# Newest block first on ScalarE, the gate's silu in one group, the finished features rounded behind the last head, the last panel turned by half

## The chip, the cores and the metric

One core of a Trainium2 chip runs the whole program. TensorE (PE) does the matmuls and transposes, ScalarE (ACT) the activations and copies, VectorE (DVE) the elementwise work and reductions, GpSimd (POOL) some elementwise work, and SyncE (SP) issues the DMAs. The metric is the device time of one execution, in microseconds (us); lower is better.

## What is computed

Two transformer blocks on 1024 tokens of width 1024, float32 in and out. The change lies in the last three stages of the second block: multi-head latent attention and the output product.

```
    q = (rms_norm(c_q, q_a_norm) @ w_uq).reshape(B, L, MLA_HEADS, QK_HEAD)
    kv = (rms_norm(c_kv, kv_a_norm) @ w_ukv).reshape(B, L, MLA_HEADS, QK_NOPE + V_HEAD)
    k_nope, v = kv[..., :QK_NOPE], kv[..., QK_NOPE:]
    k = jnp.concatenate([k_nope, k_r], axis=-1)
    q = rms_norm(q, q_norm)
    k = rms_norm(k, k_norm)
...
        s = jnp.einsum('bqhd,bkhd->bhqk', qb, k).astype(jnp.float32) * scale
        mask = cid[None, :] <= qc[:, None]
        s = jnp.where(mask[None, None], s, neg)
        p = jax.nn.softmax(s, axis=-1).astype(v.dtype)
        return jnp.einsum('bhqk,bkhd->bqhd', p, v)
...
    return o * jax.nn.silu(z)
...
    y = jnp.concatenate([y_conv, y_mla, y_ret], axis=-1)      # 256 + 512 + 256 features
    h = h + y @ w_out[l]
```

y has 256 features of the convolution, 512 of the attention (8 heads of 64) and 256 of the retention.

Float32 products are made of three matmuls on operands rounded to a shorter float32 format (F32R): high by high, high by low, low by high. "Rounding" a tensor means a copy to its high part on ScalarE and the difference, its low part, on VectorE.

## The kernel before

Every engine has its own instruction stream, written out by hand; semaphores (counted steps) are the only order between engines. Weights come in panels. A panel is loaded (`sp_weights`, line 285), rounded on ScalarE (`act_split`, line 294) and on VectorE (`dve_split`, line 300), and multiplied by `pe_dense` (lines 313 to 315): per half of 512 tokens 8 blocks k of input features, 3 matmuls each, so 24 matmuls of 512 columns a half and 48 a panel. The three stages that matter:

**Latent stage.** Its last four panels `mz` 0 to 3 (the gate z) have matmuls enough to hide other work behind, which is put into *slots* between the k blocks. `slot_at` names the blocks after which a slot comes: 3 slots in each of the halves 0 to 2, 4 in each of the halves 3 to 5, 7 in the halves 6 and 7. Slots 0 to 16 start one *item* each: item m = 0 to 7 is the query product of a block of 128 tokens (12 matmuls of 384 columns, line 2376), item m = 8 to 16 the key and value product of a block (6 matmuls of 512 columns, line 2386; the last block has 16 tokens). An item goes through steps s = 0 to 3, one slot apart: s = 0 is the product on TensorE and on ScalarE its copy out of PSUM (lines 2400, or 2416 and 2417) and the square (2402, 2419); s = 1 the sum of squares on VectorE (2431, 2445 and 2447) and the square root on ScalarE (2405, 2423); s = 2 the normalisation on VectorE; s = 3 the rope on GpSimd. In one slot every engine does its part of up to four items, and `head_slots` lists them **oldest item first**. An item's two PSUM banks come from a ring of four, so TensorE's item m needs the copies of item m - 2. The results are stored to HBM (lines 2471, 2475) and, when all stores have landed, loaded again by head (`head_sp`, lines 2483 to 2485). `silu(j - 1)` of the gate runs at the start of panel mz j on ScalarE (line 2239). The halves 6 and 7 hold the preparation of head 0: its first step transposes the loaded queries (tile `qhd`, line 326).

**Attention stage.** For each of 8 heads 14 units (pairs of a key block and a query half): three score matmuls (2606 to 2608), exp on ScalarE (2654), one value matmul (2617). Behind the units of head h lies the preparation of head h + 1; behind head 7 lies nothing.

**Output stage.** The 8 feature blocks y (k = 0, 1 convolution, in `yb`; 2 to 5 attention, in `zf2`; 6, 7 retention, transposed from `rb`) are rounded into XH and XL (lines 2734, 2737, 2757), then 8 panels of `w_out_2` are multiplied, the residual `hr` is added (line 2765), the panel is transposed back (`turn`, line 326), copied to `ot` (line 2744) and stored (line 2846). Feature block 5 needs the end of head 7: a reciprocal on VectorE (line 2668) and two products on GpSimd.

## Time and profile before

| | us |
|---|---|
| median of 3 runs | 2192.44 (2191.07 to 2192.71) |
| the profiled execution | 2190.02 |
| its span, first to last record | 2188.1 |
| TensorE busy in it | 2045.3 (93%) |
| ScalarE, VectorE, GpSimd busy | 699.9, 1039.6, 381.5 |
| mean granted TensorE clock | 0.967 of 2.4 GHz |

TensorE is busy for 93% of the span, so a gain has to come from its idle stretches, from its time at the lower clock, or from what precedes and follows its work. A busy matmul overlaps the next one: one of 512 columns is recorded with 0.39 us while they start 0.23 us apart.

### The profile page before, as it was taken

The numbers are of one execution on the slowest core, as the hardware profiler recorded it, in microseconds if no ns is written. First come the engines' busy times: TensorE is split into PE (matmuls) and PEld (weight loads), VectorE is DVE, ScalarE is ACT, GpSimd is POOL, SyncE is SP. The second block draws the span as 40 slices with busy tenths as digits, with TensorE's granted clock in tenths as the row PEclk, the third lists the DMA queues.
The fourth block names the chain that finished last, engine by engine and source line by source line (L and its number), as shares of the span: only waits on it lengthen the run. The fifth ranks groups of instructions, "written<-read, shape, count | busy, mean of one in ns | idle before, by whom it ended". The sixth has DMA issues, their size and how long they took to land.

```text
span 2188.1 us, 24747 instructions
## 1 busy us (share of the span) xinstructions
PE 2045.3 (93%) x9965; PEld 1672.3 (76%) x9965; DVE 1039.6 (48%) x1700; ACT 699.9 (32%) x1204; POOL 381.5 (17%) x436
## 2 busy tenths in 40 slices
PE   7988799959998999999999999997989999799998
PEld 6766588847786888888888888775978897576677
DVE  5666734644545333333333335436454436566541
ACT  4435121234434212212112123334111126555421
POOL 3142201630030000000000002343051316000100
PEclk9989899969999999999999999998999999899999
DMA  4133232122111111111111111111310132411123
GB/s 140 39 95 117 77 100 79 55 72 58 49 46 46 49 49 49 49 49 48 46 51 40 50 56 58 38 39 52 117 38 20 49 106 97 134 44 30 39 77 96
DMA packets 195721, 139.18 MB, mean 64 GB/s; under 512 B 35016, under 2 KB 180680, under 8 KB 195096
## 3 DMA queue, kind: packets, MB, share of 16 engines
q1 hardware_dynamic: 195608, 137.60, 20.9%
q8 instruction: 79, 1.29, 0.3%
q14 instruction: 34, 0.28, 0.0%
HBM read 109.22 MB, written 28.36 MB: 63 GB/s over the span
## 4 chain that ended last, share of the span: by engine, by line
PE 79%; DVE 10%; ACT 5%; issue 2%; POOL 2%; DMA 1%; SPq 0%; ACTq 0%; DVEq 0%; POOLq 0%
PE ps L313 21%; PE ps L314 20%; PE ps L315 20%; PE ps L326 3%; PE ps L2617 3%; PE ps L517 2%; PE ps L1174 1%; DVE wlo L300 1%; PE ps L2547 1%; PE ps L2606 1%; PE ps L2607 1%; PE ps L2608 1%; DVE fm L910 1%; DVE xl L1442 1%; PE ps L1158 1%
## 5 line engine op out<-in xcount | busy, mean ns | idle before, releaser
L313 PE MATMUL ps<-xh,whi 128*128 128x512 f32 (+2 forms) x1728 | 694.3, 402 | 34.2 <-DVE wlo L300 18.4
L314 PE MATMUL ps<-xl,whi 128*128 128x512 f32 (+2 forms) x1728 | 674.8, 391 | 0.0
L315 PE MATMUL ps<-xh,wlo 128*128 128x512 f32 (+2 forms) x1728 | 671.3, 388 | 0.0
L313 PEld LDWEIGHTS ps<-xh,whi 128*128 128x128 f32 x1728 | 331.9, 192 | 109.7 <-issue 24.4
L315 PEld LDWEIGHTS ps<-xh,wlo 128*128 128x128 f32 x1728 | 331.2, 192 | 66.1
L314 PEld LDWEIGHTS ps<-xl,whi 128*128 128x128 f32 x1728 | 331.6, 192 | 61.4 <-issue 3.1
L294 ACT ACTIVATE whi<-wraw 128x1024 fp32r<-128x1024 f32 (+2 forms) x151 | 147.0, 974 | 360.6 <-PE ps L315 347.9
L300 DVE TENSOR_TENSOR wlo<-wraw,whi 128x1024 fp32r<-128x1024 f32 (+2 forms) x151 | 192.9, 1278 | 115.7 <-ACT whi L294 115.6
L313 PE MATMUL ps<-ffh,whi 128*128 128x512 f32 x512 | 199.4, 389 | 0.0
L314 PE MATMUL ps<-ffl,whi 128*128 128x512 f32 x512 | 199.3, 389 | 0.0
L315 PE MATMUL ps<-ffh,wlo 128*128 128x512 f32 x512 | 199.2, 389 | 0.0
L1508 DVE TENSOR_TENSOR hT<-hT,ps 128x512 f32<-128x512 f32 x128 | 87.7, 687 | 178.7 <-PE ps L315 178.7
L1412 POOL COPY acc<-sqp 128x512 f32<-128x512 f32 x6 | 3.5, 613 | 677.8 <-ACT sqp L1599 677.8
L1468 ACT ACTIVATE rr<-rr 128x512 f32<-128x512 f32 x64 | 40.5, 633 | 247.3 <-DVE rr L1487 247.3
L315 PEld LDWEIGHTS ps<-ffh,wlo 128*128 128x128 f32 x512 | 96.1, 188 | 20.1
L313 PEld LDWEIGHTS ps<-ffh,whi 128*128 128x128 f32 x512 | 96.1, 188 | 20.1
L314 PEld LDWEIGHTS ps<-ffl,whi 128*128 128x128 f32 x512 | 96.1, 188 | 19.8
L1487 DVE SCALAR_TENSOR_TENSOR rr<-ps,rst 128x512 f32<-128x512 f32 x64 | 44.2, 691 | 133.4 <-PE ps L315 133.4
L2617 PE MATMUL ps<-pt,vm 128*128 128x512 f32 (+4 forms) x224 | 89.8, 485 | 0.0
L1489 DVE TENSOR_TENSOR ffl<-rr,ffh 128x512 fp32r<-128x512 f32 x64 | 44.4, 693 | 87.2 <-ACT ffh L1472 87.2
L2654 ACT ACTIVATE pt<-ps 128x512 f32<-128x512 f32 (+4 forms) x112 | 52.9, 473 | 74.1 <-PE ps L2608 73.7
L1415 POOL TENSOR_TENSOR acc<-acc,sqp 128x512 f32<-128x512 f32 x42 | 60.2, 1462 | 39.4 <-ACT sqp L1599 39.4
(437 smaller groups left out, 2590.8 us busy)
## 6 DMA issues: line engine op xcount, KB each, us to landing
wraw<-w_in SPq DMA_DIRECT2D x47, 512.0 KB, 3.7
wraw<-w_up SPq DMA_DIRECT2D x32, 512.0 KB, 4.1
wraw<-w_down SPq DMA_DIRECT2D x32, 512.0 KB, 3.4
xt<-x SPq DMA_DIRECT2D x8, 512.0 KB, 7.0
wraw<-w_o SPq DMA_DIRECT2D x16, 256.0 KB, 3.0
xr<-x SPq DMA_DIRECT2D x8, 512.0 KB, 4.4
wraw<-w_ple_gate SPq DMA_DIRECT2D x8, 512.0 KB, 4.3
h_d<-hT SPq DMA_DIRECT2D x8, 512.0 KB, 3.3
```

Source lines behind the costliest of these rows:

```text
L294: act.activation(whi[i % 2][:, 0:n], raw[i % 2][:, 0:n], ACT.Copy).then_inc(*act_w.up(i))
L300: dve.tensor_tensor(wlo[i % 2][:, 0:n], raw[i % 2][:, 0:n], whi[i % 2][:, 0:n].bitcast(F32), ALU.subtract).then_inc(*dve_w.up(i))
L313: pe.matmul(out, h, xh[:, k, c0:c1_], start=(k == 0), stop=False)
L314: pe.matmul(out, h, xl[:, k, c0:c1_], start=False, stop=False)
L315: mm = pe.matmul(out, l, xh[:, k, c0:c1_], start=False, stop=(k == nk - 1))
L326: t = pe.transpose(out, in_, ident[0:p, 0:p])
L1415: pool.tensor_tensor(acc, acc, sq[:], ALU.add).then_inc(*done.up("sum", i))
L1487: dve.scalar_tensor_tensor(r[:], tile("up", g, f, c0), 0.0, RST[:, s], ALU.max, ALU.mult).then_inc(*dve_ml.up("ev", "up", g, f, c0))
L1489: dve.tensor_tensor(ffL[g % 2][:, f, s], r[:], ffH[g % 2][:, f, s].bitcast(F32), ALU.subtract).then_inc(*dve_ml.up("ff low", g, f, c0))
L1508: dve.tensor_tensor(d, d, tile("down", g, n, c0), ALU.add).then_inc(*dve_ml.up("ev", "down", g, n, c0))
L2617: pe.matmul(tile("o", h, hf)[:, c0:512], values_of(h, x), pts[j % 4][0:n_keys(x), 0:512 - c0], start=(x == 0), stop=(x == last_x[hf])).the ...
L2654: act.activation(pts[j % 4][0:n_keys(x), 0:512 - c0], tile("unit", h, u)[0:n_keys(x), 0:512 - c0], ACT.Exp).then_inc(*act_at.up("exp", h, u))
```

## The change

1. **Newest first on ScalarE.** In a slot ScalarE now takes the block steps in reverse: first the copies and the square of the new item, then the square root of the item before. The other engines keep the order oldest first.
2. **The gate's silu together.** silu 0 to 2 run at the start of half 7, silu 3 right after, so that the functions of ScalarE change less often.
3. **The mask rows (`kaug`, `qaug`)** are loaded after item 14's store, once TensorE has done the last item's product, and no longer after all stores.
4. **Rounding behind the last head.** The transposes of blocks 6 and 7 lie behind the units 0 to 3 of head 7, the rounding of the blocks 6, 7, 2, 3, 4 behind its units 0 to 9; blocks 0, 1, 5 follow at its end, first half first. `pe_dense` takes the blocks in the order 6, 7, 2, 3, 4, 0, 1, 5. Some tiles of heads 1, 3, 5, 7 move so that the places in XH and XL are free (`y_place`).
5. **Last panel turned by half.** The transposes of panel 6 lie between the halves of panel 7, those of panel 7's first half behind its second half's fourth block; each half of an output panel is stored by itself.

```
-            for m, s in head_slots[n] if n < n_head_slots else ():
+            block_steps = head_slots[n] if n < n_head_slots else []
+            for m, s in block_steps[::-1] if newest_first else block_steps:
                 heads(m, s)
...
-            else:
-                silu(j - 1)
...
             for hf in range(2):
-                in_slots(2 * j + hf, lambda m, s: heads_act(act, w, m, s), lambda *step: prepare_act(act, w, 0, *step))
+                if (j, hf) == (3, 1):
+                    for done in range(3):
+                        silu(done)
+                in_slots(2 * j + hf, lambda m, s: heads_act(act, w, m, s), lambda *step: prepare_act(act, w, 0, *step), True)
...
-    ql = [M("ql0", 40.125, [T], F32R), X("ql1", 12416, [T], F32R)]
-    pts = [X(f"pt{i}", 16512 + 2048 * i, [512]) for i in range(4)]
+    ql = [M("ql0", 40.125, [T], F32R), X("ql1", 33280, [T], F32R)]
+    pts = [X(f"pt{i}", 37440 + 2048 * i, [512]) for i in range(4)]
...
+    y_order = [6, 7, 2, 3, 4, 0, 1, 5]
+    y_place = [0, 1, 7, 3, 4, 2, 5, 6]
+    early = [(k, hf) for ks in ((6, 7), (2,), (3,), (4,)) for hf in range(2) for k in ks]
+    def y_turn_pe(pe, w, k, hf):
+        p = take(w, "max", ("y", k, hf), (dve_ou, ("low", k, 512 * hf)))
...
+    def y_high_act(act, w, k, hf):
...
+    def y_low_dve(dve, w, k, hf):
...
                 if h < 7:
                     for step in prepare[u]:
                         prepare_pe(pe, w, h + 1, *step)
+                elif u < 4:
+                    y_turn_pe(pe, w, *early[u])
...
+                elif u < len(early):
+                    y_high_act(act, w, *early[u])
+        for k in (0, 1, 5):
+            y_high_act(act, w, k, 0)
         summed(7, 1)
...
+                if h == 7 and u < len(early):
+                    y_low_dve(dve, w, *early[u])
+        for k in (0, 1, 5):
+            if k > 0:
+                w.wait_ge(*pe_at.end())
+            y_low_dve(dve, w, k, 0)
         for n in range(4):
             inverse(3, 1, n)
...
+        for n in range(8):
             for hf in range(2):
...
+                pe_dense(pe, w, pe_ou, ("final", n), OUT0 + n, dve_ou, XX, y_ready, cols=HALVES[hf:hf + 1], order=y_order, place=y_place,
+                         behind=last_turn if (n, hf) == (7, 1) else None)
+                if (n, hf) == (7, 0):
+                    turn(6, 0)
+                    turn(6, 1)
+            if 0 < n < 7:
+                turn(n - 1, 0)
+                turn(n - 1, 1)
+        turn(7, 1)
...
+            if m == 14:
+                w.wait_ge(*pe_la.at("kv", NB, 1))
+                sp.dma_start(ak[96:AUG, :], ap["kaug"]).then_inc(*ld_aug.up("k"))
+                sp.dma_start(aq[96:AUG, :], ap["qaug"]).then_inc(*ld_aug.up("q"))
...
-        sp.dma_start(ak[96:AUG, :], ap["kaug"]).then_inc(*ld_aug.up("k"))
-        sp.dma_start(aq[96:AUG, :], ap["qaug"]).then_inc(*ld_aug.up("q"))
...
-            w.wait_ge(*act_ou.at("out", n, 1))
-            sp.dma_start(out3[:, :, 128 * n:128 * n + 128], ot[n % 3][:]).then_inc(*st_out[n % 3].up(n))
+            for hf in range(2):
+                bs = slice(4 * hf, 4 * hf + 4)
+                w.wait_ge(*act_ou.at("out", n, hf))
+                sp.dma_start(out3[:, bs, 128 * n:128 * n + 128], ot[n % 3][:, bs, :]).then_inc(*st_out[n % 3].up(n, hf))
```

How the rows move. ScalarE at the start of panel mz 2, before the change (vm and qk are the copies of an item, sq its square, the mst row the square root of the item before, whi the panel's rounding, zf the gate):

```order
L2419 ACTIVATE sq_224<-qk_221 128x512
L294 ACTIVATE whi_73<-wraw_71 128x1024
L2239 ACT_TABLE_LOAD
L2239 ACTIVATE zf_212<-zf_212 128x1024
L2423 ACT_TABLE_LOAD
L2423 ACTIVATE mst<-mst,eps 128x8
L2416 ACTIVATE vm<-ps,mst 128x2x2x64
L2417 ACTIVATE qk_222<-ps,mst 128x4x64
L2416 ACTIVATE vm<-ps,mst 128x2x2x64
L2417 ACTIVATE qk_222<-ps,mst 128x4x64
L2419 ACTIVATE sq_225<-qk_222 128x512
L2423 ACTIVATE mst<-mst,eps 128x8
```

The same place now:

```order
L2422 ACTIVATE sq_224<-qk_221 128x512
L2426 ACTIVATE mst<-mst,eps 128x8
L294 ACTIVATE whi_73<-wraw_71 128x1024
L2419 ACTIVATE vm<-ps,mst 128x2x2x64
L2420 ACTIVATE qk_222<-ps,mst 128x4x64
L2419 ACTIVATE vm<-ps,mst 128x2x2x64
L2420 ACTIVATE qk_222<-ps,mst 128x4x64
L2422 ACTIVATE sq_225<-qk_222 128x512
L2426 ACTIVATE mst<-mst,eps 128x8
```

Between the square of one item and the copies of the next there is now only the root of an item whose sum was asked for one slot earlier, and the panel's rounding; two table loads and the silu are gone from there.

TensorE from the last values of head 7 to the first output panel, before (pt is the exp of a unit, rb the retention features):

```order
L2617 MATMUL ps<-pt_252,vm 128x192
L2617 MATMUL ps<-pt_253,vm 128x64
L326 MATMUL ps<-ident,rb 128x128 x16
L313 MATMUL ps<-xh,whi_74 128x512
L314 MATMUL ps<-xl,whi_74 128x512
L315 MATMUL ps<-xh,wlo_76 128x512
```

And now:

```order
L2649 MATMUL ps<-pt_252,vm 128x192
L2649 MATMUL ps<-pt_253,vm 128x64
L314 MATMUL ps<-xh,whi_74 128x512
L315 MATMUL ps<-xl,whi_74 128x512
L316 MATMUL ps<-xh,wlo_76 128x512
```

The 16 transposes are gone from this place; they stand in four groups of 4 behind the first four units of head 7.

## Rows read from the trace of the kernel before

**Rows 1.** Windows: us, busy PE, PEld, DVE, ACT, POOL; clock, DMA share, GB/s.

```profile
1805.90:1873.20 67.30, 59.31 (x272) 48.24 (x271) 43.78 (x75) 44.97 (x87) 33.94 (x65) 0.97 0.28 99
1867.10:1870.50 3.40, 3.13 (x8) 2.48 (x9) 2.14 (x5) 2.34 (x7) 0.00 (x0) 0.50 0.29 116
1884.20:1891.00 6.80, 4.79 (x17) 3.94 (x18) 1.49 (x2) 1.37 (x2) 1.86 (x2) 0.50 1.08 390
2061.00:2078.80 17.80, 17.80 (x77) 12.14 (x76) 3.39 (x4) 8.96 (x19) 2.55 (x2) 1.00 0.00 0
2078.80:2097.40 18.60, 15.31 (x65) 11.99 (x66) 15.85 (x22) 10.54 (x19) 2.89 (x2) 0.91 0.07 19
454.00:477.80 23.80, 12.32 (x52) 10.60 (x52) 11.01 (x30) 6.45 (x11) 8.76 (x6) 0.50 0.44 155
```

**Rows 2.** Timeline of PE in the slots: start, duration, line, shape, idle before.

```profile
1867.37 0.76 PE L2386 MATMUL ps<-ukH,ckH 128*128 128x512 f32 x1 [4.02 <-ACT qk L2417]
...
1872.82 0.39 PE L2386 MATMUL ps<-ukL,ckH 128*16 128x512 f32 x1
```

**Rows 3.** Timeline of ACT at the start of panel mz 2 and in one slot.

```profile
1860.74 1.04 ACT L294 ACTIVATE whi<-wraw 128x1024 fp32r<-128x1024 f32 x1
1861.80 1.28 ACT L2239 ACT_TABLE_LOAD   x1
...
1864.17 1.28 ACT L2423 ACT_TABLE_LOAD   x1
...
1868.91 0.30 ACT L2423 ACTIVATE mst<-mst,eps 128x8 f32<-128x8 f32 x1 [1.02 <-DVE mst L2447]
1869.12 0.46 ACT L2416 ACTIVATE vm<-ps,mst 128x256 f32<-128x256 f32 x1
...
1870.70 0.63 ACT L2419 ACTIVATE sq<-qk 128x512 f32<-128x512 f32 x1
```

**Rows 4.** Timeline of DVE in the same slot.

```profile
1869.24 0.20 DVE L2450 RECIPROCAL mst<-mst 128x8 f32<-128x8 f32 x1 [0.37 <-ACT mst L2423]
...
1872.09 0.23 DVE L2447 TENSOR_SCALAR mst<-mst 128x8 f32<-128x8 f32 x1
```

**Rows 5.** Timeline of DVE in the output stage: the residual sums of two panels.

```profile
2132.59 0.69 DVE L2765 TENSOR_TENSOR hr<-hr,ps 128x512 f32<-128x512 f32 x1 [4.87 <-PE ps L315]
...
2139.05 0.69 DVE L2765 TENSOR_TENSOR hr<-hr,ps 128x512 f32<-128x512 f32 x1 [2.73 <-PE ps L315]
2144.61 0.69 DVE L2765 TENSOR_TENSOR hr<-hr,ps 128x512 f32<-128x512 f32 x1 [4.87 <-PE ps L315]
```

**Rows 6.** The chain that ended last: start, us, one query item on PE.

```profile
1811.11 2.08 PE ps L2376 x12
```

**Rows 7.** Timelines of ACT, DVE, SP and PE from the last item to head 0.

```profile
1876.01 0.45 ACT L2416 ACTIVATE vm<-ps,mst 16x256 f32<-16x256 f32 x1
...
1880.09 0.67 DVE L2455 TENSOR_TENSOR qk<-qk,mst 16x512 f32<-16x512 f32 x1
...
1882.58 0.40 SPq L2483 DMA_DIRECT2D qhd<-q_d  x1
...
1886.21 1.06 PE L326 MATMUL ps<-ident,qhd 128*104 128x128 f32 x4 [6.03 <-POOL qh L2365]
```

**Rows 8.** Timelines of ACT and DVE between attention and the first output panel.

```profile
2081.13 2.17 ACT L2734 ACTIVATE xh<-zf 128x512 fp32r<-128x512 f32 x4
...
2079.46 3.39 DVE L2668 RECIPROCAL den<-den 128x128 f32<-128x128 f32 x4 [5.25 <-ACT den L2641]
```

**Rows 9.** Timelines of DVE, ACT and SP at the end, then one output store alone.

```profile
2180.68 0.69 DVE L2765 TENSOR_TENSOR hr<-hr,ps 128x512 f32<-128x512 f32 x1 [4.87 <-PE ps L315]
...
2181.17 2.09 ACT L2744 ACTIVATE ot<-ps 128x512 f32<-128x512 f32 x4 [10.93 <-PE ps L326]
...
2182.28 1.37 SPq L2846 DMA_DIRECT2D out<-ot  x2
...
out<-ot SPq DMA_DIRECT2D x1, 512.0 KB, 4.0
```

More of the change, by code:

```diff
@@ L300, in dve_split, with pe_dense @@
             dve.tensor_tensor(wlo[i % 2][:, 0:n], raw[i % 2][:, 0:n], whi[i % 2][:, 0:n].bitcast(F32), ALU.subtract).then_inc(*dve_w.up(i))
-    def pe_dense(pe, w, done, key, i, emptier, x, ready, nk=8, cols=HALVES, tl=0, step=128, behind=None, every=4, kind="dense"):
+    def pe_dense(pe, w, done, key, i, emptier, x, ready, nk=8, cols=HALVES, tl=0, step=128, behind=None, every=4, kind="dense", order=range(8), place=range(8)):
         xh, xl = x
@@ L308, in pe_dense @@
             w.wait_ge(*dve_w.at(i))
-            for k in range(nk):
+            for n, k in enumerate(order[0:nk]):
                 for ev in ready(k, c0):
                     w.wait_ge(*ev)
+                xk = place[k]
                 h, l = (t[i % 2][:, tl + step * k:tl + step * k + 128] for t in (whi, wlo))
-                pe.matmul(out, h, xh[:, k, c0:c1_], start=(k == 0), stop=False)
-                pe.matmul(out, h, xl[:, k, c0:c1_], start=False, stop=False)
-                mm = pe.matmul(out, l, xh[:, k, c0:c1_], start=False, stop=(k == nk - 1))
-                if k == nk - 1:
+                pe.matmul(out, h, xh[:, xk, c0:c1_], start=(n == 0), stop=False)
+                pe.matmul(out, h, xl[:, xk, c0:c1_], start=False, stop=False)
+                mm = pe.matmul(out, l, xh[:, xk, c0:c1_], start=False, stop=(n == nk - 1))
+                if n == nk - 1:
                     mm.then_inc(*done.up(*key, c0))
-                if k % every == every - 1 and behind:
+                if n % every == every - 1 and behind:
                     behind()
@@ L2618, in values @@
                       ).then_inc(*pe_at.up("values", j))
-        for u in range(first_slot[8] - n_head_slots, nu):
-            for step in prepare[u]:
-                prepare_pe(pe, w, 0, *step)
         for h in range(8):
@@ L2729, in output_act, with turn @@
-    def output_act(act, w):
-        w.wait_ge(*pe_at.end())
-        for hf in range(2):
-            for k in range(6):
-                w.wait_ge(*(ld_y.end() if k < 2 else pool_at.at("y", k - 2, hf)))
-                act.activation(XH[:, k, 512 * hf:512 * hf + 512], y_of(k)[:, 512 * hf:512 * hf + 512], ACT.Copy).then_inc(*act_ou.up("high", k, 512 * hf))
-            for k in range(6, 8):
-                w.wait_ge(*pe_ou.at("y", k, hf))
-                act.activation(XH[:, k, 512 * hf:512 * hf + 512], tile("y", k, hf), ACT.Copy).then_inc(*act_ou.up("high", k, 512 * hf))
+        def turn(n, hf):
+            w.wait_ge(*dve_ou.at("ev", "final", n, 512 * hf))
+            p = take(w, "misc", ("out", n, hf), (act_ou, ("out", n, hf)))
+            pe_turn(pe, [(p[:, 128 * m:128 * m + 128], hr[n % 3][:, 512 * hf + 128 * m:512 * hf + 128 * m + 128]) for m in range(4)]).then_inc(*pe_ou.up("out", n, hf))
@@ L2751, in output_dve @@
     def output_dve(dve, w):
-        w.wait_ge(*pe_at.end())
-        for hf in range(2):
-            cs = slice(512 * hf, 512 * hf + 512)
-            for k in range(8):
-                w.wait_ge(*act_ou.at("high", k, 512 * hf))
-                dve.tensor_tensor(XL[:, k, cs], y_of(k)[:, cs] if k < 6 else tile("y", k, hf), XH[:, k, cs].bitcast(F32), ALU.subtract
-                                  ).then_inc(*dve_ou.up("low", k, 512 * hf))
+        y_low_dve(dve, w, 0, 1)
+        y_low_dve(dve, w, 1, 1)
+        dve_split(dve, w, OUT0 + 1)
+        y_low_dve(dve, w, 5, 1)
         for n in range(8):
-            dve_split(dve, w, OUT0 + n + 1)
+            if n > 0:
+                dve_split(dve, w, OUT0 + n + 1)
             for c0 in (0, 512):
```

57 lines of the change are left out of this document (29 added, 28 removed).

## The prediction

> **What bounds the kernel now.** I read the page first: TensorE is busy for 93% of the span, so the question is where the other 7% lies. The timeline of TensorE, read for idle stretches over the three stages that the diff touches, and the windows over those stages answer it; the timelines of the other engines then say who is late. Three places stand out.
>
> The slots with items, from the first item's first matmul (1805.9) to the last's last (1873.2), take 67.3 us, in which TensorE is busy for 59.3: 8.0 us idle, all in eight stalls ahead of key items, the longest 4.02 us, all ended by ScalarE's copies [rows 1, 2]. After the longest the granted clock is 0.50, the lower of its two levels (1.2 GHz), for 3.4 us [rows 1]. ScalarE itself waits there: in one slot it starts the root of item m - 1, which has waited 1.02 us for VectorE, then copies item m, then squares it, and only then can VectorE sum that square [rows 3, 4]. So the two engines take turns: root to root is 3.45 us (root and copies from 1868.91, square to 1871.33, VectorE's sum to 1872.32, handover). TensorE's own slot is shorter: 6 matmuls of the panel and 6 of the item at 0.232 us each (24 matmuls lie between the second and third residual sum, 5.56 us [rows 5]), 2.8 us. At the start of panel mz 2 ScalarE also has the panel's rounding, two table loads of 1.28 and the silu, 4.7 us before the next copies [rows 3]: that is the 4.02 us stall.
>
> From the last item to head 0, TensorE has 7.0 us of panel matmuls and then waits 6.03 us for head 0's queries; the clock is 0.50 for 6.8 us [rows 1, 7]. The record names GpSimd's copy of the mask rows as releaser, but the transpose needs only the loaded queries; the load was issued at 1882.58 and takes 3.6 us to the transpose [rows 7]. That is a chain: last copies, sum, root, normalisation to 1880.76, store, landing, load.
>
> From the last value matmul (2078.8) to the end of the first output panel (2097.4) pass 18.6 us for 48 matmuls worth 11.1, with the mean clock at 0.91 [rows 1]. At the very end, the last sum starts at 2180.68 and the span ends at 2188.1: 7.4 us of sum, transposes, four copies and two 512 KB stores behind each other [rows 9].
>
> **The change part by part.** All sums are against the profiled execution, span 2188.1 (2190.02 with what lies around it), which is 2.4 us under the median of the runs; I carry the difference over to the median.
>
> *Slots.* What TensorE has to do from first to last item: 111 panel matmuls of 0.232 (five halves less the three blocks before slot 0), 25.7; 8 query items of 2.08 [rows 6], 16.7; 9 key items of 6 times 0.232, 12.5; the small transposes and restarts about 1.4. Sum 56.3. With the new order ScalarE copies item m while VectorE still works on m - 2 and m - 1, and the root needs a sum that is one slot old. The remaining loop is VectorE's slot (1869.24 to 1872.32 less its idle 0.86, 2.2 us) and the handover to the root and back (0.37): 2.6 us, under TensorE's 2.8 [rows 4]. The whole stage agrees: VectorE is busy for 43.8 us, 17 handovers add 6.3, sum 50, under 56.3; ScalarE's 45.0 lose the four table loads and two silu, 7.2, leaving 38 [rows 1, 3]. The panel's rounding (1.04 on ScalarE) is once more than a slot holds, but TensorE is two banks ahead, 2.7 us (two slots less the item's own matmuls, less 1.5 for copies). So I take the stage as TensorE's: 67.3 - 56.3 = **11.0 gained**. It contains the 8.0 idle, 1.7 of lower clock and the eight restarts. The moved silu hides in half 7, where ScalarE has nothing else; its cover is gone only if the group (1.28 + 3 times 1.06) outlasts that half's 5.6 us.
>
> *What is late next.* The chain to head 0's queries does not shrink as much. Before: copies start 2.8 after the last product, then 2.2 to the end of the square, 2.6 to the normalised rows, 1.8 to the load, 3.6 to the transpose: 13.0 [rows 7]. Now ScalarE is behind by some 2.0 instead of 2.8, but newest first puts the root of item 15, VectorE's end of item 15 (1.3) and a panel result (0.6) ahead of item 16's sum: 2.6 grows to 4.5. Sum 14.2, against cover of 6.9: the idle stretch grows to 7.3, **1.2 lost**. Bounds: 12 if nothing stands in the way, 15.5 if the lag stays 2.8 and GpSimd's earlier mask copies slow VectorE. Moving the mask rows ahead costs nothing that waits (SP waits for a product that TensorE has finished when item 14 is normalised) and gives nothing, since they were not what the transpose waited for. The lower clock after this idle stretch stays, as it was.
>
> *Head 7.* TensorE gets 16 transposes. A pair of residual sums with 8 transposes between them lies 6.46 apart, without them 5.56 [rows 5]: 0.11 each, 1.8 at most, less where a transpose fills the tail of a float32 value matmul. ScalarE is busy for 9.0 of head 7's 17.8 us [rows 1] and gets 10 roundings of 0.54 [rows 8], 14.4 in all, still under TensorE's 19. **1.5 lost**, bounds 1.0 and 3.0 (ScalarE's part bunched in the first ten units).
>
> *Start of the output.* The first panel can start right behind the last value: 48 matmuls, 11.1, and 0.2 for the switch, instead of 18.6: **7.3 gained**, of which 1.6 is lower clock that follows no idle stretch any more. Its cover: blocks 0, 1, 5 of the first half are needed 3.5 us after the start, their rounding takes 1.6 on ScalarE. Block 5 of the second half waits for VectorE's reciprocals (3.4 [rows 8]), now behind three roundings, then GpSimd 1.3 and both roundings: some 8.5 us after the last value, needed at 10.4. If that cover fails, the price is the excess only.
>
> *End.* TensorE's last matmul comes 12 transposes later, **1.3 lost**. Behind it stand the sum 0.7, four transposes to the copy 0.7, one copy 0.6, the issue, and one half store. A whole store alone lands in 4.0 [rows 9]; the last two, 1.05 MB queued behind each other, fill the 5.8 us from 2182.28 to the end, some 2 of which are issue and landing, so 256 KB are worth 0.9 and a half store 3.1. With 0.8 from landing to the end of the span: 5.9, against 7.4; without the stragglers of that lone store 5.0. **1.5 to 2.4 gained**, so 0.8 net in the middle.
>
> A rule that speaks against this edit: the Trainium skill, "DMA: Bandwidth & Descriptors" (Rules for kernel authors; Anatomy of one DMA), wants few large transfers, since each costs 2.0 us and only then bytes over 436 GB/s. By it a half store is 2.6 against 3.2 for a whole one, 0.6 less, and the end would lose 0.7 instead of gaining 0.8, an estimate of 2177.5 for the whole. The trace shows no half store; its whole ones speak for some 275 GB/s, at which the half saves more.
>
> Sum: 11.0 - 1.2 - 1.5 + 7.3 + 0.8 = 16.4. 2192.44 - 16.4 = 2176.0.
>
> **The rivals.** (a) *VectorE becomes the bound of the slots.* Its products run longer while GpSimd works on the rope (GpSimd is busy for 34 of the 67 us [rows 1]); at 3.2 us a slot TensorE would wait 0.4 in the key slots and more at a panel's start, and 11.0 shrinks to about 7: 2180. Against it: VectorE has 6 us of slack in the sum above. (b) *More is gained at head 0.* If the chain takes 12 us and the clock does not fall ahead of the queries, 2.2 and up to 2 more: 2172. (c) *The slots' gain goes into the wait for the queries*, because their release is set by something that I take for late and is not (the DMA queue, weight loads): only the output's parts remain, 2186. The loads of the next weight panels stand on the same queue, but the one at item 13 was issued long before. (d) *Slower by the clock.* The trace has a stretch of 23.8 us at 0.50, with TensorE half idle, in another stage [rows 1]. If the rearranged head 7 and output made TensorE run like that, each us would cost half a us; it decides at 33 us of it, and 60 us would give 2206. Against it: head 7 is at 1.00 with no idle time [rows 1], and in the stretches at 0.50 that the rows show TensorE had just been idle for several us or was idle half the time. (e) *It does nothing*: TensorE's stalls are ended by something else than ScalarE's order, and the early rounding costs in head 7 what it saves behind: 2192. The releasers in all eight stalls speak against it.
>
> **How the numbers follow.** The forecast, 2173 to 2179 by the bounds of the chain, of head 7 and of the end, has 0.64; (a) 2179 to 2183 0.14; (b) 2170 to 2173 0.15; (c) 0.04; (d) 0.02; (e) 0.01. A range from 2171 to 2181.5 leaves out (c) to (e), a third of (a) and a third of (b), about 0.17. 0.2%, 4.4 us, is about what a measurement of this kernel can tell from no change: faster 0.97, same 0.01, slower 0.02.
>
> **What would show it.** Right: no TensorE stall over 0.3 us in the item slots, the last item's product 11 us earlier; an idle stretch near 7.3 us ahead of the first query transpose; head 7 some 19 us long; the output's first matmul right behind the last value at clock 1.00, first panel 11.3 us; span's end 5 to 6 us behind the start of the last sum. Wrong: stalls in the slots ended by VectorE (a), a chain to the queries of over 16 us (c), ScalarE late in head 7's units so that TensorE waits for exp, or granted clock at 0.50 in a stretch without an idle one ahead of it (d).

## The result, and the profile after

The changed kernel takes 2176.82 us (median of 4 runs, 2175.46 to 2179.26), the kernel before, run beside it, 2192.57 (4 runs, 2191.07 to 2193.73): ratio 0.9930, 95% interval 0.9913 to 0.9947. It is faster by 0.7%. Repeated on another occasion (5 runs of the change, 9 of the kernel before) the medians are 2177.18 and 2189.43, ratio 0.9941 (0.9927 to 0.9955). The two ratios agree within their intervals, and the difference of the medians was 15.8 us once and 12.3 once.

The traces show where much of the spread lies: ahead of the first item, where both kernels are the same, the first item's first matmul starts anywhere from 1805.6 to 1810.6 us in the 14 traces of this case. The stretches with a granted clock of 0.50 ahead of it add up to 112.6 to 126.3 us there, but the start follows their sum only loosely (1805.9 and 1807.9 us in the two traces with the smallest sum, 1808.3 and 1809.5 in the two with the largest), so the clock is at most a part of the cause. Stages are therefore compared by their lengths, not by their place in the span. The page of the profiled run begins:

```profile
span 2177.4 us, 24757 instructions
PE 2041.1 (94%) x9965; PEld 1671.1 (77%) x9965; DVE 1040.0 (48%) x1700; ACT 695.1 (32%) x1200; POOL 384.5 (18%) x436
```

Windows over the stages that the change touches (us, busy PE, PEld, DVE, ACT, POOL; clock, DMA share, GB/s): items, last product to head 0's first scores, heads 0 to 6, head 7, last value to first output panel, and the longest stretch at 0.50.

```profile
1808.93:1867.94 59.01, 56.90 (x272) 47.53 (x271) 40.23 (x71) 37.79 (x81) 34.80 (x65) 1.00 0.29 104
1867.94:1900.06 32.12, 24.57 (x105) 18.99 (x104) 20.69 (x42) 12.49 (x22) 4.19 (x2) 0.84 0.44 152
1900.06:2056.88 156.82, 152.10 (x711) 107.58 (x711) 97.23 (x172) 81.58 (x161) 17.55 (x15) 0.99 0.18 49
2056.88:2076.34 19.46, 19.46 (x93) 13.70 (x91) 11.08 (x15) 14.83 (x31) 1.67 (x2) 1.00 0.00 0
2076.34:2087.71 11.37, 11.37 (x49) 9.21 (x50) 10.47 (x12) 4.55 (x7) 4.26 (x3) 1.00 0.04 12
1876.80:1887.00 10.20, 5.37 (x19) 4.47 (x20) 2.58 (x3) 1.38 (x2) 3.04 (x2) 0.50 0.81 287
```

Against [rows 1]: the items take 59.0 instead of 67.3 with 2.1 idle instead of 8.0; head 7 takes 19.5 instead of 17.8, without idle time; the first output panel ends 11.4 behind the last value instead of 18.6, at clock 1.00.

TensorE's timeline shows which stalls are left in the items (and last, the wait for head 0's queries):

```profile
1855.58 0.48 PE L2389 MATMUL ps<-ukH,ckH 128*128 128x512 f32 x1 [0.44 <-ACT qk L2420]
1859.50 0.47 PE L2389 MATMUL ps<-ukH,ckH 128*128 128x512 f32 x1 [0.87 <-ACT qk L2420]
1862.80 0.47 PE L2389 MATMUL ps<-ukH,ckH 128*128 128x512 f32 x1 [0.26 <-ACT qk L2420]
...
1881.63 1.06 PE L327 MATMUL ps<-ident,qhd 128*104 128x128 f32 x4 [6.73 <-DMA qhd<-q_d]
```

A fourth stall of 0.54 stands ahead of 1866.4. The row that names ScalarE as releaser doesn't say why ScalarE was late. Its own timeline does: the first copies of items 11 and 12, then the root of item 13, then an undisturbed slot (root, copies, square):

```profile
1853.87 0.47 ACT L2419 ACTIVATE vm<-ps,mst 128x256 f32<-128x256 f32 x1 [1.38 <-DMA q_d<-qk]
...
1857.79 0.48 ACT L2419 ACTIVATE vm<-ps,mst 128x256 f32<-128x256 f32 x1 [1.50 <-DMA q_d<-qk]
...
1864.50 0.30 ACT L2426 ACTIVATE mst<-mst,eps 128x8 f32<-128x8 f32 x1 [1.17 <-DVE mst L2450]
...
1866.99 0.30 ACT L2426 ACTIVATE mst<-mst,eps 128x8 f32<-128x8 f32 x1
1867.20 0.46 ACT L2419 ACTIVATE vm<-ps,mst 128x256 f32<-128x256 f32 x1
...
1868.78 0.63 ACT L2422 ACTIVATE sq<-qk 128x512 f32<-128x512 f32 x1
```

In the undisturbed slot the root waits for nothing, and root to root is 2.50 us where [rows 3] had 3.45: what the prediction said of the new order holds. But items 11 and 12 wait for a store. An item's rows stand in one of five buffers (qk[m % 5]), so item 11's copies need the landed store of query item 6, and that store needs GpSimd's rope of item 6. GpSimd's timeline has the cause of the delay: ropes without a pause, and between those of items 5 and 6 the 2.0 us memset of the ones in the value tile:

```profile
1845.61 0.46 POOL L962 TENSOR_TENSOR qk<-qk,rt 128x128 f32<-128x128 f32 x1
1846.01 2.02 POOL L2463 MEMSET vm<- 128x2304 f32 x1
1848.00 0.67 POOL L955 TENSOR_TENSOR rt<-qk,c 128x128 f32<-128x128 f32 x1
...
1854.52 0.45 POOL L962 TENSOR_TENSOR qk<-qk,rt 128x128 f32<-128x128 f32 x1
```

At the end, the last sum on VectorE, the last copy on ScalarE, and the last two stores on SP (issue; KB each, median us to landing), against [rows 9]: from the start of the last sum to the end 4.8 us instead of 7.4.

```profile
2172.55 0.69 DVE L2794 TENSOR_TENSOR hr<-hr,ps 128x512 f32<-128x512 f32 x1 [6.21 <-PE ps L316]
2173.98 0.60 ACT L2775 ACTIVATE ot<-ps 128x512 f32<-128x512 f32 x1 [3.56 <-PE ps L327]
2170.44 4.53 SPq L2879 DMA_DIRECT2D out<-ot  x2
out<-ot SPq DMA_DIRECT2D x2, 256.0 KB, 2.3
```

### The profile page after: what moved, and what is told of

It is laid out like the page before. It is cut to its first block, busy times and chain, and to the rows that moved or that the text cites. A ratio compares the mean times of both kernels' runs of the same rounds, so it can differ in the third digit from the quotient of the medians.

```text
span 2177.4 us, 24757 instructions
## 1 busy us (share of the span) xinstructions
PE 2041.1 (94%) x9965; PEld 1671.1 (77%) x9965; DVE 1040.0 (48%) x1700; ACT 695.1 (32%) x1200; POOL 384.5 (18%) x436
## 4 chain that ended last, share of the span: by engine, by line
PE 79%; DVE 10%; ACT 3%; POOL 3%; issue 2%; DMA 2%; SPq 0%; DVEq 0%; ACTq 0%; POOLq 0%
PE ps L314 21%; PE ps L315 20%; PE ps L316 20%; PE ps L327 4%; PE ps L2649 3%; PE ps L518 2%; DVE wlo L300 1%; PE ps L1175 1%; PE ps L2550 1%; PE ps L2638 1%; PE ps L2639 1%; PE ps L2640 1%; DVE fm L911 1%; DVE xl L1443 1%; PE ps L1159 1%
## 5 line engine op out<-in xcount | busy, mean ns | idle before, releaser
L314 PE MATMUL ps<-xh,whi 128*128 128x512 f32 (+2 forms) x1728 | 694.6, 402 | 31.9 <-DVE wlo L300 18.5
```

Source lines behind the costliest of these rows:

```text
L314: pe.matmul(out, h, xh[:, xk, c0:c1_], start=(n == 0), stop=False)
```

## The experiments

Each kernel below was timed against the kernel before, on one of four occasions (the kernel before took 2192.57 beside the change, 2192.22 beside the next four, 2189.66 beside the four after them, 2189.43 beside the last four), so rows are compared by ratio and not by time. An interval reaches 0.0012 to 0.0017 to either side, so ratios less than about 0.002 apart can't be told from each other, and the verdicts rest on lengths of stages, taken from the starts and ends of TensorE's rows in one profile of each kernel. The last row of the table but one is the changed kernel profiled again: its stages agree with the first profile within 0.1 us, also in the stretches at 0.50. That agreement is not the rule: up to the output stage "whole stores" has the same instructions as the change, and its chain is 0.9 longer and its prepare 0.4 shorter. Where that comes from is told under whole stores. "Chain" is the last item's last product to head 0's first query transpose, "prepare" from there to head 0's first scores, "end" the last output matmul to the span's end.

| kernel | items | chain | prepare | heads 0 to 6 | head 7 | end | first item to span's end | time us | ratio (95%) |
|---|---|---|---|---|---|---|---|---|---|
| before | 67.3 | 13.0 | 18.1 | 156.7 | 17.8 | 7.5 | 382.2 | 2192.57 | 1 |
| change | 59.0 | 13.7 | 18.4 | 156.8 | 19.5 | 4.9 | 368.4 | 2176.82 | 0.9930 (0.9913 to 0.9947) |
| silu in place | 63.8 | 12.9 | 18.3 | 156.7 | 19.5 | 4.9 | 372.2 | 2180.37 | 0.9955 (0.9941 to 0.9969) |
| oldest first | 66.1 | 13.0 | 18.7 | 157.0 | 19.5 | 4.9 | 375.2 | 2182.99 | 0.9965 (0.9951 to 0.9978) |
| output part only | 67.3 | 13.9 | 17.7 | 158.4 | 19.5 | 4.9 | 377.8 | 2184.25 | 0.9964 (0.9952 to 0.9976) |
| ones late | 57.4 | 13.5 | 17.7 | 156.7 | 19.5 | 4.9 | 365.8 | 2177.18 | 0.9936 (0.9924 to 0.9949) |
| whole stores | 59.1 | 14.6 | 18.0 | 156.9 | 19.5 | 6.1 | 370.3 | 2181.09 | 0.9959 (0.9945 to 0.9972) |
| turns last | 59.1 | 13.6 | 18.6 | 156.9 | 19.5 | 6.7 | 369.1 | 2176.49 | 0.9941 (0.9928 to 0.9955) |
| last sum first | 59.0 | 13.1 | 17.1 | 158.0 | 19.5 | 4.9 | 367.7 | 2177.86 | 0.9951 (0.9935 to 0.9967) |
| fill | 59.0 | 13.8 | 15.9 | 158.2 | 19.5 | 4.9 | 367.4 | 2176.26 | 0.9934 (0.9922 to 0.9947) |
| early queries | 59.1 | 10.1 | 20.3 | 155.4 | 19.5 | 4.9 | 365.4 | 2176.38 | 0.9935 (0.9921 to 0.9949) |
| two fills | 59.2 | 14.4 | 17.5 | 155.2 | 19.5 | 4.9 | 366.8 | 2174.01 | 0.9925 (0.9912 to 0.9939) |
| change again | 59.1 | 13.6 | 18.5 | 156.8 | 19.5 | 4.9 | 368.5 | 2177.18 | 0.9941 (0.9927 to 0.9955) |
| together | 57.4 | 9.1 | 19.8 | 155.5 | 19.5 | 4.9 | 362.2 | 2172.19 | 0.9920 (0.9906 to 0.9933) |

**Silu in place.** The change with the silu of each panel at the next one's start.

```diff
+            if j > 0:
+                silu(j - 1)
...
-                if (j, hf) == (3, 1):
-                    for done in range(3):
-                        silu(done)
```

> The change without its grouping of the silu: ScalarE takes the newest block first, but each panel's silu stands at the start of the next panel, with its two table loads (1.28 us each) and 1.06 of its own. Theory of the prediction (ScalarE's place is what TensorE waited for): 3.6 us stand ahead of the copies at the start of panels mz 1, 2 and 3, and TensorE is two banks (2.7 us less 1.5 for the copies, so some 1.2) ahead, so each start costs about 2.4 us of stall that the change does not have, but only mz 2 lies in the key items where TensorE waits at once; I expect 2 to 5 us more than the change in the stretch from first to last item, span and time by as much, ratio to before 0.994 to 0.995. Rival (the silu was hidden anyway, newest first does it all): the stretch stays within 0.5 us of the change's 59.0.

Measured: 63.8 us for the items, 4.8 more than the change, within the first theory's 2 to 5; the ratio, 0.9955, is just above the expected 0.994 to 0.995. (The expectation takes the 1.5 for the copies off a second time: the 2.7 had them off already. The range holds all the same.) TensorE's longest stall, and ScalarE's rows ahead of it:

```profile
1863.96 0.65 PE L2388 MATMUL ps<-ukH,ckH 128*128 128x512 f32 x1 [2.60 <-ACT qk L2419]
...
1860.01 1.28 ACT L2241 ACT_TABLE_LOAD   x1
1861.31 1.06 ACT L2241 ACTIVATE zf<-zf 128x1024 f32<-128x1024 f32 x1
1862.27 0.46 ACT L2418 ACTIVATE vm<-ps,mst 128x256 f32<-128x256 f32 x1
```

**Oldest first.** The other half taken away.

```diff
-                in_slots(..., lambda *step: prepare_act(act, w, 0, *step), True)
+                in_slots(..., lambda *step: prepare_act(act, w, 0, *step))
```

> The change without newest first: ScalarE takes the oldest block first in a slot, silu grouped at the end. Theory of the prediction: ScalarE's and VectorE's turns follow each other again, 3.45 us a key slot against TensorE's 2.8, so the nine key items take about 6 us more than in the change (first to last item some 65 us instead of 59.0), and the chain from the last item to head 0's queries is about 1.0 shorter, 12.7 instead of 13.7: net 5 us more, ratio about 0.995. Rival (silu and table loads were what TensorE waited for): within 1 us of the change.

Measured: 66.1 for the items, 1.1 more than expected; the chain is 0.7 shorter. In this order the grouping of the silu alone gains only 1.2 us (67.3 to 66.1), since a stall nearly as long as before's (3.67 against 4.02) stays at the start of panel mz 2: TensorE, then ScalarE's root, which waits for a sum, and VectorE's rounding ahead of that sum, which waits for ScalarE's:

```profile
1864.93 0.77 PE L2389 MATMUL ps<-ukH,ckH 128*128 128x512 f32 x1 [3.67 <-ACT qk L2420]
...
1863.03 0.30 ACT L2426 ACTIVATE mst<-mst,eps 128x8 f32<-128x8 f32 x1 [3.33 <-DVE mst L2450]
...
1859.73 1.23 DVE L300 TENSOR_TENSOR wlo<-wraw,whi 128x1024 fp32r<-128x1024 f32 x1 [2.85 <-ACT whi L294]
```

Newest first alone gains 3.5 (67.3 to 63.8), the grouping alone 1.2, both 8.3: either hides the other, and 3.6 of the gain need both.

**Output part only.** Both edits above together: the slots are as before.

> The slots as before (oldest first, silu in place), the rest of the change kept: early rounding in head 7, turned halves, half stores, mask rows ahead. Theory of the prediction: 67.3 us from first to last item as before, 13.0 to the queries, and the terms of head 7 (-1.7 lost), of the output's start (7.2 gained) and of the end (1.0 gained) stay as they are: 6.5 us under before, ratio 0.997. Rival (the parts depend on each other, for instance half a us is given back through the granted clock): over 1.5 us away from that.

Measured: 67.3 for the items, as before; head 7, the start of the output and the end as in the change to within 0.02 us. From first item to end 4.4 us under before instead of 6.5: the chain was 0.9 longer (VectorE's small addition to item 16's sum took 1.11 us instead of 0.22, see whole stores), and heads 0 to 6 took 1.7 more, where a stretch at 0.50 behind the wait for head 1's queries was 6.8 us instead of 3.4. By time it is 8.0 under before. The three terms of the output stand; the sum of the stages misses by 2.1 through the chain and the clock, so the rival's bound of 1.5 is passed.

**Ones late.** GpSimd's memset behind its last rope (its copies of the mask rows then wait for it).

```diff
-        if (m, s) == (NB, 0):
+        if (m, s) == (NB - 1, 3):    # behind rope(...) of this item
             w.wait_ge(*pe_la.at("q", NB - 1, 1))
             pool.memset(vm[:, :, :, 1, :], 1.0).then_inc(*pool_la.up("ones"))
```

> The change with one instruction of GpSimd moved: the memset of the ones in the value tile (2.0 us), which stands between the ropes of query items 5 and 6, goes behind the rope of item 7. New theory for the 2.7 us that the slots missed: ScalarE's copies of items 11 and 12 wait 1.38 and 1.50 us for the stores of query blocks 6 and 7 (five buffers), and these stores wait for GpSimd's ropes. With the ropes of items 6 and 7 some 2 us earlier both waits vanish, TensorE's stalls at 1855.1 and 1858.6 (0.44 and 0.87) with them, and with the lag gone part of the two later ones (0.26, 0.54): from first to last item 57.3 to 57.9 instead of 59.0, ratio to before 0.0006 lower than the change's. Rival (VectorE sets the pace, rival a of the prediction: its products take 0.95 instead of 0.69 while GpSimd works): the waits on the stores turn into waits on VectorE's sums and the stretch stays at 59.0 within 0.4.

Measured: 57.4, within the first theory's 57.3 to 57.9. Item 11's copies wait for nothing any more, item 12's 0.54 instead of 1.50, and the stalls of 0.44 and 0.87 are gone:

```profile
1853.23 0.46 ACT L2420 ACTIVATE vm<-ps,mst 128x256 f32<-128x256 f32 x1
...
1856.69 0.48 ACT L2420 ACTIVATE vm<-ps,mst 128x256 f32<-128x256 f32 x1 [0.54 <-DMA q_d<-qk]
...
1863.40 0.30 ACT L2427 ACTIVATE mst<-mst,eps 128x8 f32<-128x8 f32 x1 [1.15 <-DVE mst L2451]
```

Two stalls stay, 0.28 and 0.51, behind the panel's rounding and the root that waits 1.15 for VectorE: that is what is left of rival (a). By time the step can't be told from the change (ratio 0.9936 beside 0.9930 and 0.9941).

**Whole stores.** One 512 KB store a panel.

```diff
-            for hf in range(2):
-                bs = slice(4 * hf, 4 * hf + 4)
-                w.wait_ge(*act_ou.at("out", n, hf))
-                sp.dma_start(out3[:, bs, 128 * n:128 * n + 128], ot[n % 3][:, bs, :]).then_inc(*st_out[n % 3].up(n, hf))
+            w.wait_ge(*act_ou.at("out", n, 1))
+            sp.dma_start(out3[:, :, 128 * n:128 * n + 128], ot[n % 3][:]).then_inc(*st_out[n % 3].up(n, 1))
```

> The change with one store of 512 KB for each output panel instead of two of 256 KB; the turning of halves stays. Measured from the start of the last residual sum to the span's end. Theory of the prediction (256 KB are worth 0.9 us, a half store lands in 3.1, a whole one in 4.0): 0.9 us later than the change, more if the last two whole stores queue behind each other. By the Trainium skill's page DMA: Bandwidth & Descriptors (2.0 us and bytes over 436 GB/s) it would be 0.6 later, an estimate. Rival (the store's size is of no weight, the end is set by issue and landing): within 0.3.

Measured: 1.2 us later (6.1 instead of 4.9). The DMA view of the last store (GB/s in 40 slices of the last 8.5 us, then the issue):

```profile
GB/s 0 0 0 0 0 0 0 0 0 0 0 0 0 0 0 0 0 0 0 0 0 0 0 0 0 65 294 292 289 296 292 289 292 280 80 0 0 0 0 0
out<-ot SPq DMA_DIRECT2D x1, 512.0 KB, 3.2
```

Whole it lands in 3.2 us, halves in 2.3. While these stores move, the DMA view has some 290 GB/s, at which 256 KB are worth 0.9 us, the difference of the two. The Trainium skill, "DMA: Bandwidth & Descriptors" (Anatomy of one DMA), states its fit of 2.0 us and bytes over 436 GB/s for DMAs that GpSimd issues; these are issued by SyncE. Worked out from it, an estimate, a whole store takes 3.2 and a half 2.6. The trace agrees on the whole one and not on its parts: 1.8 us of bytes at 290 GB/s and 1.4 of the rest, and 2.3 for the half. The 4.0 of [rows 9], from mid-stage, does not recur at the very end.

This run also shows why the chain differs where the instructions don't. Here, then in the change, GpSimd's first copy of the mask rows and VectorE's normalisation of item 16 beside it:

```profile
1877.06 1.17 POOL L2366 CAST kh<-ak 24x1040 fp32r<-24x1040 f32 x1 [20.35 <-DMA aq<-qaug]
1877.24 1.53 DVE L2458 TENSOR_TENSOR qk<-qk,mst 16x512 f32<-16x512 f32 x1
...
1875.65 3.15 POOL L2366 CAST kh<-ak 24x1040 fp32r<-24x1040 f32 x1 [20.68 <-DMA aq<-qaug]
1875.48 0.67 DVE L2458 TENSOR_TENSOR qk<-qk,mst 16x512 f32<-16x512 f32 x1
```

Where GpSimd's copy starts first, VectorE's product takes 1.53 us instead of 0.67, and item 16's store is issued 9.08 us behind the last product instead of 8.23, the query load as much later; where VectorE starts first, GpSimd's copy takes 3.15 instead of 1.05. Two fills has the first case too (chain 14.4); output part only and oldest first have it between GpSimd's second copy and the small addition to item 16's sum (1.11 and 1.07 us instead of 0.22). In the kernel before, the mask rows are loaded later, GpSimd's copies start when VectorE has done item 16, and neither is lengthened. From its issue to its landing the query load takes 3.3 to 3.6 us in every run in which it is issued in the old place.

**Turns last.** Panels 6 and 7 turned behind the last matmul, half stores kept (the diff takes back `last_turn` and the calls `turn(6, 0)`, `turn(6, 1)` ahead of it).

> The change with the turning of panels 6 and 7 as in the kernel before: panel 6's eight transposes and all of panel 7's eight stand behind the last matmul; half stores stay. Theory of the prediction: TensorE's last matmul comes 1.3 us earlier, but the copies of four halves and their stores then stand behind each other: from the last matmul's result to the end about 7 us instead of 4.9, net 0.5 to 1.0 us slower than the change. Rival (the transposes ahead of the last matmul cost as much as they save): within 0.3.

Measured: the output's matmuls end 1.33 us earlier (12 transposes at 0.11), the end takes 6.7 instead of 4.9: 0.5 slower, at the lower bound of the expectation, and too little for the times to show (ratio 0.9941).

**Last sum first.** VectorE's order in the last item slots, from the slot of item 16's sum on (`from_slot=17` in VectorE's call alone).

```diff
-            for m, s in block_steps[::-1] if newest_first else block_steps:
+            for m, s in block_steps[::-1] if newest_first or n >= from_slot else block_steps:
```

> The change with VectorE taking the newest block first in the last two item slots: the sum over item 16's square ahead of the normalisation of item 15. It bears on the chain to head 0's queries (13.7 us from the last product to the first transpose). In the change the root of item 16 waits 2.30 us for its sum, behind VectorE's end of item 15 and a panel result. Theory: the root comes 1.2 us earlier, item 16's normalisation then waits for item 15's, and the rows are ready 0.5 to 1.0 earlier: 12.7 to 13.2 instead of 13.7. Rival (the queue's landing and issue set the load, not the normalised rows): no change of the chain.

Measured: chain 13.1, 0.6 shorter; item 16's root waits 1.13 instead of 2.30, and its store is issued 0.46 earlier. Prepare is 1.3 shorter too, since the stretch at 0.50 there is 6.8 us instead of 10.2; but the one in head 0 is 6.8 instead of 3.4, and heads 0 to 6 take 1.2 more. Net 0.8.

**Fill.** 24 matmuls whose result nothing uses, ahead of head 0's first transpose.

```diff
+                        if n == n_head_slots:
+                            p = take(w, "misc", ("fill",), (pe_la, ("fill",)))
+                            for _ in range(24):
+                                t = pe.matmul(p[:, 0:512], whi[(IN20 + 16 + 7) % 2][:, 0:128], XH[:, 0, 0:512], start=True, stop=True)
+                            t.then_inc(*pe_la.up("fill"))
```

> The change with 24 matmuls more (128x512, 0.23 us each, result unused) on TensorE ahead of head 0's first transpose, where it stands idle for 6.7 us. It tests what the idle stretch costs beyond itself: in the change the granted clock is 0.50 from 1876.8 to 1887.0, so the 5.4 us behind the idle stretch run at half speed. Theory (the lower clock comes of the idle time): clock 1.00 throughout, the stretch from the first query transpose to the first scores of head 0 takes 15.7 to 16.2 us instead of 18.4, and the time is 2.2 to 2.7 us under the change's. Rival one (that stretch is bound by the chain over ScalarE and VectorE, not by TensorE): clock 1.00 but 18.0 to 18.4. Rival two (the lower clock comes of something else): a stretch at 0.50 all the same.

Measured: prepare 15.9 instead of 18.4, at 1.00 throughout. But behind the next idle time, 2.79 us ahead of head 1's queries, the clock is at 0.50 for 6.8 us instead of 3.4. Windows over both:

```profile
1881.50:1897.40 15.90, 14.78 (x71) 11.12 (x69) 12.36 (x23) 7.10 (x10) 1.12 (x2) 1.00 0.26 104
1899.20:1906.00 6.80, 6.11 (x21) 4.66 (x21) 1.49 (x2) 3.02 (x6) 0.00 (x0) 0.50 0.63 164
```

1.0 is left of 2.5. Rivals one and two are out for this stretch; how much of the loss in head 0 comes of the fill, a single profile can't say, since output part only and last sum first have 6.8 us there without one.

**Early queries.** Head 0's query load at item 14 (`head_sp` then leaves it out for head 0).

```diff
             if m == 14:
                 w.wait_ge(*pe_la.at("kv", NB, 1))
+                for mq_ in range(NB):
+                    w.wait_ge(*st_qk[mq_ % 5].at(mq_))
+                sp.dma_start(qhd[0][:, :, 0:96], q_d[:, :, 0:96].rearrange("b p d -> p b d")).then_inc(*ld_q[0].up(0))
```

> The change with head 0's query load issued at item 14, when the stores of the query blocks have landed, instead of behind the store of the last key block. It tests how much of the 6.7 us idle stretch belongs to the order of the loads. Theory: the two query transposes and the six panel matmuls between them and the key transposes (0.53 each group of four at full clock, 0.70 a slot, some 2.5 us) move ahead of the idle stretch, which then stands ahead of the first key transpose and is 4.2 us long; from the last item's last product to head 0's first scores 29.3 to 30.2 instead of 32.1, of which some comes from a shorter stretch at clock 0.50. Rival (the load beside the last key stores delays these, on the same queues): 31.5 or more.

Measured: 30.4 from the last product to head 0's scores instead of 32.1, just above the expected 30.2. The idle time is two pieces, 3.16 ahead of the queries and 2.86 ahead of the keys, not one of 4.2: SP's and TensorE's timelines show the load issued early, but it lands only 6.2 us after its issue (3.5 in the change): a key store and a 512 KB weight load were issued ahead of it and still under way, and the mask rows and two more key stores follow behind it.

```profile
1866.12 0.38 SPq L285 DMA_DIRECT2D wraw<-w_out  x1
1868.20 0.32 SPq L2478 DMA_DIRECT2D k_d<-qk  x1
1868.84 0.37 SPq L2860 DMA_DIRECT2D qhd<-q_d  x1
...
1875.15 0.62 PE L327 MATMUL ps<-ident,qhd 128*104 128x128 f32 x4 [3.16 <-DMA qhd<-q_d]
1880.47 0.96 PE L327 MATMUL ps<-ident,khd 128*96 128x128 f32 x4 [2.86 <-DMA khd<-k_d]
1899.18 0.62 PE L327 MATMUL ps<-ident,qhd 128*104 128x128 f32 x4 [2.82 <-DMA qhd<-q_d]
```

The last row is the wait for head 1's queries, as long as in the other kernels. Here no stretch at 0.50 follows it: the clock is 1.00 through heads 0 to 6, which take 155.4 us instead of 156.8, and no matmul was added. The only stretch at 0.50 between the first item and the output's end, 3.4 us, lies behind the stall of 2.86 in prepare. From first item to end this run is 3.0 under the change, more than any other single edit.

**Two fills.** The 24 matmuls, and 10 ahead of head 1's first transpose, on head 0's keys and queries.

> The change with the 24 extra matmuls ahead of head 0's first transpose and 10 more (result unused, 2.3 us) ahead of head 1's first transpose, where TensorE stands idle for 2.7 us. In the run with the 24 alone the first stretch at 0.50 vanished (2.5 us gained up to head 0's first scores) but 1.4 was given back in head 0, where the stretch at 0.50 behind the second idle time took 6.8 us instead of 3.4. Theory (both are the price of idle time): no stretch at 0.50 behind 1874 us, head 0's start to head 7's start 155.0 to 155.5 instead of 156.8, and from the first item to the end 4.0 us under the change's 368.4. Rival (the chip gives the lower clock at some later point whatever TensorE does): a stretch of 3.4 or 6.8 at 0.50 in head 0 or 1 all the same.

Measured: heads 0 to 6 at 155.2 and clock 1.00, as expected: the wait for head 1's queries is down to 0.42 us. Up to head 0's scores only 0.2 is gained: the queries came 0.7 later than in the change, TensorE was idle for 1.95 us in spite of the fill, and the clock was at 0.50 for 3.4 us behind it. 1.7 from first item to end instead of 4.0; the theory failed for the first place. For the second it is not shown: early queries has the same single stretch before (3.4 us, starting 15.6 us behind the last product, here 15.7), left the wait of 2.82 unfilled, and has no lower clock in heads 0 to 6 either (155.4).

**Together**, with the change again beside it.

> The change with all that has gained: GpSimd's memset behind the ropes, VectorE's last sum first, head 0's queries loaded early, 16 extra matmuls ahead of head 0's first key transpose and 10 ahead of head 1's first. Theory (the parts add up, since each shortens another stretch): slots 57.4 (1.65 less than the change), last product to head 0's first scores 26.5 to 28 instead of 32.1, head 0 to head 7 155.2 instead of 156.8: 7 to 9 us from the first item to the end, time 2168 to 2170.5, ratio 0.990. Rival (they get in each other's way; what one shortens, the next waits for): 4 us or less.

> The change once more, beside the version above on the same chip. Theory: first item to end 368.4 within 1.5, since only the stretches at 0.50 vary there, ratio to before 0.993; what differs from its first profile lies ahead of the first item, where the stretches at lower clock fall differently from run to run. Rival (the times by stage are not reproducible to within 0.3 us outside the stretches at 0.50): stages differ by more, and the differences of under 1 us told of the other runs mean nothing.

Windows of the version together (items, last product to head 0's scores, heads 0 to 6), then of the change again:

```profile
1807.94:1865.29 57.35, 56.53 (x272) 47.60 (x271) 40.39 (x71) 37.88 (x81) 34.90 (x65) 1.00 0.30 108
1865.29:1894.14 28.85, 25.90 (x122) 19.91 (x120) 20.49 (x42) 12.41 (x22) 2.09 (x2) 1.00 0.51 169
1894.14:2049.66 155.52, 152.76 (x720) 108.18 (x721) 97.24 (x172) 81.27 (x161) 17.55 (x15) 1.00 0.18 50
```

```profile
1808.52:1867.58 59.06, 56.84 (x272) 47.54 (x271) 40.25 (x71) 37.72 (x81) 34.82 (x65) 1.00 0.29 104
1867.58:1899.68 32.10, 24.64 (x104) 19.05 (x104) 20.69 (x42) 12.48 (x22) 4.27 (x2) 0.84 0.44 152
1899.68:2056.52 156.84, 152.03 (x710) 107.62 (x711) 97.24 (x172) 81.46 (x161) 17.55 (x15) 0.99 0.18 49
```

Clock 1.00 in all three; 6.3 us from first item to end, under the expected 7 to 9 (28.9 up to head 0's scores, where 28 was the upper end). By time 2172.19 (expected 2168 to 2170.5) against 2177.18, on the same chip, and the ranges of their runs, 4 and 5, don't touch (the slowest of the version together is 2173.96, the fastest of the change 2175.29). It beats both kernels: 0.9920 (0.9906 to 0.9933) of before. What each part gives in it was not taken apart. The 10 extra matmuls ahead of head 1's queries may be of no use: early queries, without them, has 155.4 for heads 0 to 6.

## Why the prediction was right, point by point

The forecast was 2176.0 (range 2171 to 2181.5), measured 2176.82 and 2177.18. The mechanism and the sign hold in each part but one (the mask rows), but the sum was too large: from first item to end the trace loses 13.7 us, against 16.4. That the number came within 0.8 us is partly luck: the stages alone would have said 2178.7 (2192.44 - 13.7), and the medians of the second occasion differ by 12.3, those of the first by 15.8.

- *Slots: 11.0 predicted, 8.3 measured.* The term that was mis-sized. TensorE's own work was right (56.9 busy against 56.3), and so was VectorE's and ScalarE's loop (2.5 a slot against 2.6). The step that failed is "So I take the stage as TensorE's": it looked at the loop of ScalarE and VectorE and not at the ring of five buffers, which closes over GpSimd's rope and a store. Before, the items came slowly enough for that ring; with the slots faster, it is what is late next. Ones late shows 1.7 of the missing 2.7. 0.8 more are the two stalls behind the panel's rounding, which the prediction took to be covered by TensorE's two banks ahead.
- *Chain to the queries: 1.2 lost predicted, 0.7 measured* (13.7 against 14.2). The terms are as described, two of them a little shorter: ScalarE is 1.75 behind instead of 2.0, square to normalised rows takes 4.3 instead of 4.5; item 16's root waits 2.30 for its sum, behind the rest of item 15 and a panel result; last sum first gets 0.6 of it back. That "the lower clock after this idle stretch stays, as it was" was wrong: the stretch at 0.50 went from 6.8 to 10.2 us, of which 5.4 lie in prepare, and prepare took 0.3 more. That moving the mask rows ahead "costs nothing that waits" was wrong too. It left out that GpSimd's copies then run beside VectorE's work on item 16; in four of the runs this cost some 0.85 us on the path to the queries (two of them in the change's own order), though not in the two profiles of the change. The bound of 15.5 had named it.
- *Head 7: 1.5 lost predicted, 1.7 measured.* 16 transposes at 0.11.
- *Start of the output: 7.3 predicted, 7.2 measured.* Block 5 of the second half was ready 10.0 us behind the last value, not 8.5, and needed at 10.7: its cover held by less than a us. A later reciprocal would have cost directly.
- *End: 0.8 net predicted, 1.0 measured.* 2.6 gained against 1.5 to 2.4, for 1.6 more in the output's matmuls. The half store's 3.1 was too much (2.3). Two slips of the sum: 1.5 to 2.4 less 1.3 has 0.65 in the middle, not 0.8; and the price by the figures of the Trainium skill (0.7 lost) counted only the smaller store and not the copies that no longer stand in line. With the half store of 2.6, an estimate from its page "DMA: Bandwidth & Descriptors", in the place of 3.1 the prediction's own sum gives 2.0 gained and 0.7 net.
- *The rivals.* (a), VectorE as the bound, has its size (8.3, near its 7) and mostly not its cause: the long waits were on stores. (b) didn't come; the chain did not shrink. (c), the slots' gain lost in the wait for the queries: 0.7 of 8.3. (d) didn't come: the change's stretches at 0.50 between the first item and the output's end are two, and TensorE is idle for 6.7 and 2.7 us at or just ahead of their start. (e) is out by silu in place and oldest first, each of which gives back a part.

What stays open: why the stretch at 0.50 behind much the same idle time is 6.8 us in one run and 10.2 in another, and why one wait of 2.8 us is followed by none. Of the 2.7 us missing in the slots some 0.2 are unexplained. Whether the mask rows are better left in the old place wasn't tried by itself.

## What to carry to other kernels

When an order between two engines is loosened, follow each buffer that they write once round its ring, over every engine and store that has to release it: the next bound is often there, and an unrelated instruction on that path (here a 2.0 us memset) is the first thing to move. Try the parts of such an edit together before judging one alone: here they gained 3.5 and 1.2 apart and 8.3 together. And where the effect is under 1%, compare stages between fixed instructions in the traces: the times of one kernel spread over 4 to 6 us here, the stages of the change repeated to 0.1 us in a second profile. But read a difference of under 1 us down to the instruction before giving it a cause: the same instructions gave chains of 13.7 and 14.6, by which of two engines started first.

## What the runs showed of the hardware

- The price of idle time on TensorE reached beyond the idle time: 6.7 us of it were followed by a granted clock of 0.50 (1.2 GHz) for 5.4 us more. 24 matmuls of no use in that place, while nothing else changed, gave 2.5 us back in the stage behind it.
- How long an idle stretch was did not tell what followed. TensorE was idle for 2.6 to 2.9 us ahead of head 1's queries in 12 of the 14 profiles: eight had 3.4 us at 0.50 behind it, three had 6.8 (output part only, last sum first, fill), one had none (early queries, 2.82 us idle). So it is not shown that a fill there removes the lower clock. A shorter stretch ahead of head 0 went with a longer one in head 0 in fill and in last sum first, but not in ones late and whole stores.
- VectorE and GpSimd lengthened each other's work. Beside a GpSimd copy of 24x1040 elements that started 0.2 us earlier, VectorE's product took 1.53 us instead of 0.67 (whole stores); where VectorE had started first, the same copy took 3.15 us instead of 1.05 (the change).
- In the output stage at the end, halving a store from 512 to 256 KB took 0.9 us from its landing (3.2 to 2.3; the bytes moved at some 290 GB/s) and 1.2 from the end of the span.
